# Another order of ScalarE's and VectorE's work in the columns with table building

## The chip, the cores and the metric

The kernel runs on one core of a Trainium2 chip, in one launch. A core has five engines that run side by side and meet at semaphores: TensorE (matmul), VectorE, ScalarE, GpSimd and SyncE, each taking its own instructions strictly in order. The metric is the device time of one execution in microseconds, the median of some runs. Beside it stands one execution that the hardware profiler recorded.

## The reference, cut to what matters

A two-layer block (four gated feed-forward parts, a pooling and a convolution mixer) is followed by a block with attention, a recurrent part and, at the end, a layer of 16384 single-neuron experts. The change lies in this last layer, `peer_ffn`:

```python
s = jnp.einsum('thpk,hpnk->thpn', q, sub_keys)
top_s, top_i = lax.top_k(s, PEER_TOPK)
...
best_s, best_pos = lax.top_k(cand_s, PEER_TOPK)
idx = jnp.take_along_axis(cand_i, best_pos, axis=-1)
g = jax.nn.softmax(best_s, axis=-1)
u = jnp.take(expert_u, idx, axis=0)
v = jnp.take(expert_v, idx, axis=0)
act = jax.nn.gelu(jnp.einsum('td,thkd->thk', xc, u))
return jnp.einsum('thk,thkd->td', (g * act).astype(v.dtype), v)
```

There are 512 tokens in four tiles of 128; each token picks 8 x 16 = 128 of the 16384 experts, all in fp32 with 1024 features.

## The kernel before

For the last 384 tokens the kernel computes the layer densely. All experts lie in 128 columns of 128. In the *up* stage each column is a weight group of 512 KB that gives the activations of 128 experts for 384 tokens. In the *down* stage these are multiplied by a table of each token's expert weights, and by the second weights. The first 128 tokens are done sparsely: GpSimd gathers, for each of the 128 picks, the 128 rows that the tokens chose (`gather`, L492, 512 KB each, through a `ring` of 4 slots), and VectorE takes the dot product with the tokens (`dot`, L1371). A slot comes free with its dot, and then the next gather goes out.

A weight group passes through these steps. SyncE loads it to `raw` (four slots, L449; a load waits until the group four before it has its low part). ScalarE rounds it to `whi` (`hi`, L511), VectorE takes the rest `wlo` (`low`, L1359), both three columns (LOOK) ahead of TensorE. TensorE makes three matmuls for each of eight blocks (L1520 to L1522, 24 in a column). ScalarE applies the activation function to the result (`column`, L804: act_out) and has it stored to HBM (`store_acts`, L796).

The table for the dense tokens is built in the up stage too, in 3 batches (one for each token tile) of 16 chunks of 8 tokens. A chunk rides on one up column. VectorE writes two one-hot tensors (`rows`, L1458 hot_m and L1459 hot_n). ScalarE scales hot_m by the weights, eight instructions (`weigh`, L825: hot_w). TensorE multiplies hot_n by hot_w, 8 matmuls, 16 passes in the trace (`sums`, L1811), and ScalarE writes the sums to the table `spread` in two halves (`take_rows`, L833). hot_m, hot_n, hot_w and the banks of the sums are double. The semaphore hot_used counts finished sums: the one-hot tensors of chunk c+2 wait for the sums of c.

The order of work is written out by hand for each engine. After a batch of 16 chunks stands a gap of 8, 8 and 16 plain columns (GAPS), in which the 8 MB of `spread` are spilled to HBM (L853; in the last gap L856 and L857). The next batch's first `weigh` waits for the spill. The 128 dots are spread over chunks and gaps; after the last of them the first tokens' activations can be computed. TensorE runs a column and then that chunk's sums.

Of the kernel before, what the change touches and what calls it, by code (L numbers as in the profile page):

```python
# [107 lines left out]
CHUNKS = P // TC  # L108
# [14 lines left out]
def at(c, i, m):  # L123

    return c if i is None else i * m + c
# [7 lines left out]
def build(nc, stream, ada, c_rows, smalls, consts, smalls2, consts2, keys, u_rows, xin, out):  # L133
# [289 lines left out]
    def hot_column(of, c):  # L423
        return of[:, TC * c:TC * c + TC].unsqueeze(2).to_broadcast([P, TC, P])
# [10 lines left out]
    with nc.Block() as block:  # L435
# [66 lines left out]
        def _(act):  # L502
            def hi(c, i=None, m=0):

                if c >= n_groups:
                    return
                s = c % R
                act.wait_ge(raw_landed[s], at(16 * (c // R + 1), i, 16 * m // R))
                if c >= R:
                    act.wait_ge(pe_groups, at(c - R + 1, i, m))  # L510
                act.activation(whi[:, s, :, :], raw[:, s, :, :], ACT.Copy).then_inc(hi_ready, 1)  # L511
# [286 lines left out]
            def column(m, i, first=True):  # L798
                if first:
                    hi(up + m + LOOK, i, 4)  # L800
                act.wait_ge(pe_groups, at(up + m + 1, i, 4))
                if m >= 4:
                    act.wait_ge(acts_stored[m % 4], at(16 * (m // 4), i, 16))
                act.activation(act_out[:, m % 4, :], psum[4 + m % 4][:, 0:TD], ACT.Gelu_apprx_tanh).then_inc(gelu_done, 1)  # L804
                if m:
                    store_acts(m - 1, i)

            def columns_run(m0, n):

                if m0 == 0:  # L810
                    for m in range(4):
                        column(m, None)
                    m0, n = 4, n - 4
                with act.Fori(0, n // 4) as i:
                    for m in range(m0, m0 + 4):
                        column(m, i)

            def weigh(c):

                s = c % 2  # L820
                act.wait_ge(hot_mark, c + 1)
                if c >= 2:
                    act.wait_ge(hot_used, c - 1)
                for k in range(TC):
                    ins = act.activation(hot_w[:, s, k, :], hot_m[:, s, k, :], ACT.Copy, scale=pick_w[:, TC * c + k:TC * c + k + 1])  # L825
                ins.then_inc(weights_ready, 1)

            def take_rows(c):

                act.wait_ge(hot_used, c + 1)  # L830
                for half in range(2):
                    k = TC * (c % CHUNKS) + 4 * half
                    act.activation(spread[:, :, k:k + 4].rearrange("p m t -> p t m"),  # L833
                                   psum[2 * (c % 2) + half][:, :].rearrange("p (t m) -> p t m", t=4), ACT.Copy).then_inc(spread_ready, 1)
# [5 lines left out]
            for j in range(DT):  # L840
                if j:
                    act.wait_ge(spilled, 16 * j)
                weigh(CHUNKS * j)
                for k in range(CHUNKS):
                    c = CHUNKS * j + k
                    hi(up + CHUNK_AT[j] + k + LOOK)
                    if k + 1 < CHUNKS:
                        weigh(c + 1)
                    column(CHUNK_AT[j] + k, None, False)
                    take_rows(c)  # L850
                act.wait_ge(spread_ready, 2 * CHUNKS * (j + 1))
                if j < DT - 1:
                    act.dma_start(expert_weights[j], spread[:, :, :]).then_inc(spilled, 16)  # L853
                    columns_run(CHUNK_AT[j] + CHUNKS, GAPS[j])
                else:
                    act.dma_start(expert_weights[j][:, 0:EARLY, :], spread[:, 0:EARLY, :]).then_inc(spilled, 16)  # L856
                    act.dma_start(expert_weights[j][:, EARLY:NK, :], spread[:, EARLY:NK, :]).then_inc(spilled_late, 16)  # L857
# [60 lines left out]
        def _(dve):  # L918
# [444 lines left out]
            def low(n=1):  # L1363
                for c in range(cursor[0], cursor[0] + n):
                    lo(c)
                cursor[0] += n

            def dot(n=1):
                for q in range(cursor[1], cursor[1] + n):
                    dve.wait_ge(ring_landed[q % RING], 16 * (q // RING + 1))  # L1370
                    dve.tensor_tensor_reduce(ring[:, q % RING, :], ring[:, q % RING, :], h_row[:, :], 1.0, 0.0, ALU.mult, ALU.add,  # L1371
                                             dots[:, q:q + 1]).then_inc(ring_used, 1)
                cursor[1] += n
# [79 lines left out]
            def rows(c):  # L1453
                s = c % 2
                if c >= 2:
                    dve.wait_ge(hot_used, c - 1)
                numbers = iota_b[:, :].unsqueeze(1).to_broadcast([P, TC, P])
                dve.tensor_tensor(hot_m[:, s, :, :], numbers, hot_column(pick[:, 1, :], c), ALU.is_equal).then_inc(hot_mark, 1)  # L1458
                dve.tensor_tensor(hot_n[:, s, :, :], numbers, hot_column(pick[:, 0, :], c), ALU.is_equal).then_inc(hot_ready, 1)  # L1459

            for j in range(DT):
                for k in range(CHUNKS):
                    rows(CHUNKS * j + k)
                    low()
                    dot(2)
                for k in range(GAPS[j] - 4 * (j == DT - 1)):
                    low()
                    dot()

            down = SEG["down"][0]  # L1470

            def out_step(m):

                dve.wait_ge(g_landed[m % 4], 16 * (m // 4 + 1))
                dve.wait_ge(a_landed[m % 4], 16 * (m // 4 + 1))
                if m >= 2:
                    dve.wait_ge(we_ready, m - 1)
                dve.tensor_tensor(we32[:, m % 2, :], act_in[:, m % 4, :], g_ring[:, m % 4, :], ALU.mult).then_inc(we_mul, 1)
                if m >= AHEAD:
                    low()  # L1480
                dve.wait_ge(we_hi_ready, m + 1)
                dve.tensor_tensor(we[:, m % WSLOTS, 1, :], we32[:, m % 2, :], we[:, m % WSLOTS, 0, :].bitcast(F32),
                                  ALU.subtract).then_inc(we_ready, 1)
# [9 lines left out]

            for k in range(4):
                low()
                dot()
                if k:
                    out_step(k - 1)
            assert cursor == [down + AHEAD, PICKS]
# [459 lines left out]
```

## Time and profile before

| | |
|---|---|
| median of 3 runs | 3652.83 us (3651.1 to 3654.18) |
| profiled execution | 3660.15 us, span 3658.2 us |
| TensorE busy | 3286.6 us (90%) |
| VectorE busy | 1987.1 us (54%) |
| ScalarE busy | 1323.1 us (36%) |
| GpSimd busy | 1357.7 us (37%) |
| granted TensorE clock, mean | 0.940 of 2.4 GHz |
| HBM traffic | 636.86 MB, mean 174 GB/s |
| up stage with its table building | about 2475 to 3125 us |

The span runs from the first to the last instruction; the profiled execution's own time is 2 us more. Busy shares are means over stages with different limits, so a stage is to be read by itself: who waits there, and for whom.

### The profile page before, as it was taken

What the parts mean: (1) busy time and instruction counts of PE and PEld (TensorE: products, weight loads), DVE (VectorE), ACT (ScalarE), POOL (GpSimd) and SP (SyncE); (2) the same over time, 40 slices, a digit from 0 to 9 for tenths busy, and PEclk for the clock granted to TensorE, in tenths of its full rate; (3) what the DMA queues carried; (4) which work ended last, traced back from release to release, by engine and by line L of the source; (5) the groups of instructions that cost most, each with busy time, mean ns of one, the idle gap of its engine ahead of it and who ended that gap; (6) DMA issues with size and microseconds to landing.
All of it is one profiled execution on the core that took longest, in us unless ns stands there. A gap on an engine that the chain in (4) does not pass through costs nothing.

```text
span 3658.2 us, 44563 instructions
## 1 busy us (share of the span) xinstructions
PE 3286.6 (90%) x15088; PEld 2804.3 (77%) x15088; DVE 1987.1 (54%) x2967; ACT 1323.1 (36%) x1959; POOL 1357.7 (37%) x654
## 2 busy tenths in 40 slices
PE   4999689998999899999788789997877778999999
PEld 3888568886888687888566578997777778888887
DVE  6552465405550435110476768775555554688887
ACT  3322233213322323222345432445545454333333
POOL 3444244443444443444222034563333332132221
PEclk9999889999999999999898699998888889999999
DMA  5554145423552222222121032455675858899997
GB/s 224 194 193 150 58 138 195 166 98 127 195 180 96 81 98 88 98 98 98 52 69 47 14 108 98 160 164 180 219 255 174 299 174 334 317 360 364 362 363 280
DMA packets 234647, 636.86 MB, mean 174 GB/s; under 512 B 22560, under 2 KB 104736, under 8 KB 233504
## 3 DMA queue, kind: packets, MB, share of 16 engines
q1 hardware_dynamic: 87408, 318.49, 25.4%
q10 hardware_dynamic: 110256, 182.59, 14.1%
q0 software_dynamic: 36864, 134.23, 11.0%
q8 instruction: 71, 1.16, 0.1%
q14 instruction: 48, 0.39, 0.0%
HBM read 580.69 MB, written 54.53 MB: 174 GB/s over the span
## 4 chain that ended last, share of the span: by engine, by line
issue 37%; PE 28%; POOL 16%; DVE 8%; ACT 7%; DMA 3%; ACTq 0%; POOLq 0%; DVEq 0%
POOL wlo L473 16%; PE bank L1850 5%; PE bank L1851 5%; PE bank L1852 5%; PE bank L1520 3%; PE bank L1522 3%; PE bank L1521 3%; DVE ring L1371 3%; ACT hot_w L825 2%; ACT spread L833 2%; DMA ring<-u_rows_dram,cell_u 2%; DVE wlo L1359 2%; DVE hot_m L1458 2%; ACT whi L511 1%; PE bank L1717 1%
## 5 line engine op out<-in xcount | busy, mean ns | idle before, releaser
L473 POOL TENSOR_TENSOR wlo<-raw,whi 128x1024 fp32r<-128x1024 f32 x394 | 1001.9, 2544 | 1467.2 <-ACT whi L511 1466.8
L1520 PE MATMUL bank<-hhi,whi 128*128 128x512 f32 (+1 forms) x2832 | 1068.3, 377 | 53.2 <-DVE wlo L1359 21.5
L1521 PE MATMUL bank<-hlo,whi 128*128 128x512 f32 (+1 forms) x2832 | 1056.0, 373 | 0.0
L1522 PE MATMUL bank<-hhi,wlo 128*128 128x512 f32 (+1 forms) x2832 | 1054.7, 372 | 0.0
L511 ACT ACTIVATE whi<-raw 128x1024 fp32r<-128x1024 f32 x599 | 633.2, 1058 | 1010.7 <-PE bank L1522 618.7
L1520 PEld LDWEIGHTS bank<-hhi,whi 128*128 128x128 f32 x2832 | 542.2, 191 | 128.9 <-DVE wlo L1359 22.5
L1521 PEld LDWEIGHTS bank<-hlo,whi 128*128 128x128 f32 x2832 | 540.8, 191 | 71.8 <-issue 1.4
L1522 PEld LDWEIGHTS bank<-hhi,wlo 128*128 128x128 f32 x2832 | 539.0, 190 | 71.8
L1359 DVE TENSOR_TENSOR wlo<-raw,whi 128x1024 fp32r<-128x1024 f32 x205 | 251.3, 1226 | 319.9 <-ACT whi L511 300.5
L925 DVE CUSTOM_DVE_ANT_0 ada_raw<-ada_raw,cond_row 128x1024 f32<-128x1024 f32 x128 | 301.3, 2385 | 155.9 <-DMA ada_raw<-ada_dram 155.7
L492 POOL DMA_INDIRECT ring<-u_rows_dram,cell_u x128 | 215.7, 1685 | 417.2 <-DVE dots L1371 400.8
L1850 PE MATMUL bank<-whi,we 128*128 128x512 f32 x768 | 299.7, 390 | 5.1 <-issue 5.1
L1851 PE MATMUL bank<-whi,we 128*128 128x512 f32 x768 | 299.5, 390 | 0.0
L1852 PE MATMUL bank<-wlo,we 128*128 128x512 f32 x768 | 299.4, 390 | 0.0
L492 POOL DMA_INDIRECT ring<-stream_dram,cell_v x128 | 139.9, 1093 | 384.8 <-DVE y L1490 358.7
L1520 PE MATMUL bank<-uhi,whi 128*128 (+1 forms) x704 | 273.9, 389 | 0.0
L1521 PE MATMUL bank<-ulo,whi 128*128 (+1 forms) x704 | 273.9, 389 | 0.0
L1522 PE MATMUL bank<-uhi,wlo 128*128 (+1 forms) x704 | 273.9, 389 | 0.0
L1811 PE MATMUL bank<-hot_w,hot_n 128*128 128x128 f32 x768 | 154.0, 383 | 118.4 <-issue 117.5
L1811 PEld LDWEIGHTS bank<-hot_w,hot_n 128*128 128x128 f32 x768 | 144.2, 289 | 132.0 <-issue 132.0
L991 DVE TENSOR_TENSOR u<-silu,bank 128x512 f32<-128x512 f32 x88 | 60.5, 687 | 302.1 <-PE bank L1522 239.2
L563 ACT ACTIVATE uhi<-u 128x512 f32 (+1 forms) x88 | 55.6, 632 | 407.1 <-DVE u L991 407.1
(244 smaller groups left out, 3817.6 us busy)
## 6 DMA issues: line engine op xcount, KB each, us to landing
raw<-stream_dram SPq DMA_DIRECT2D x599, 512.0 KB
ada_raw<-ada_dram ACTq DMA_DIRECT2D x128, 512.0 KB, 4.1
expert_acts<-act_out ACTq DMA_DIRECT2D x128, 192.0 KB
g_ring<-expert_weights ACTq DMA_DIRECT2D x128, 192.0 KB
act_in<-expert_acts ACTq DMA_DIRECT2D x128, 192.0 KB
first_raw<-ada_dram ACTq DMA_DIRECT2D x8, 1024.0 KB, 23.4
expert_weights<-spread ACTq DMA_DIRECT2D x2, 4096.0 KB, 21.0
x<-xin_dram SPq DMA_DIRECT2D x1, 2048.0 KB, 12.5
```

The costliest lines, as they stand in the source:

```text
L473: pool.tensor_tensor(wlo[:, s, :, :], raw[:, s, :, :], whi[:, s, :, :].bitcast(F32), ALU.subtract).then_inc(lo_ready, 1)
L492: pool.indirect_dma_start(ring[:, q % RING, :], None, rows, bass.IndirectOffsetOnAxis(ap=cell[:, c:c + 1], axis=0)).then_inc(ring_landed[q ...
L511: act.activation(whi[:, s, :, :], raw[:, s, :, :], ACT.Copy).then_inc(hi_ready, 1)
L925: dve.tensor_tensor_reduce(ada_raw[:, u % 2, :], ada_raw[:, u % 2, :], cond_row[:, :], 1.0, 0.0, ALU.mult, ALU.add, ada_dot[:, u % KT:u % ...
L1359: dve.tensor_tensor(wlo[:, s, :, :], raw[:, s, :, :], whi[:, s, :, :].bitcast(F32), ALU.subtract).then_inc(lo_ready, 1)
L1520: pe.matmul(bank, whi[:, s, b, :], rhi, start=start, stop=False)
L1521: pe.matmul(bank, whi[:, s, b, :], rlo, start=False, stop=False)
L1522: return pe.matmul(bank, wlo[:, s, b, :], rhi, start=False, stop=stop)
L1811: mm = pe.matmul(out, hot_n[:, s, k, :], hot_w[:, s, k, :], start=True, stop=True)
L1850: pe.matmul(bank, we[:, m % WSLOTS, 0, toks], rh, start=m == 0, stop=False, skip_group_check=True)
L1851: pe.matmul(bank, we[:, m % WSLOTS, 1, toks], rh, start=False, stop=False, skip_group_check=True)
L1852: mm = pe.matmul(bank, we[:, m % WSLOTS, 0, toks], rl, start=False, stop=last, skip_group_check=True)
```

## The change

ScalarE: in a batch the two instructions that write chunk c-1 to `spread` stand behind the next column's whi, ahead of hot_w; before, those of chunk c stood behind act_out of the same column. VectorE: the one-hot tensors of chunk c+1 are made ahead of the low part of chunk c's column; before, those of chunk c, and the batch begins with those of its first chunk. In place of two dots a chunk column has one and two by turns, and a gap column has two, every fourth one, in place of one. No instruction is added or removed; 24 of the 128 dots move from the chunk columns to the gaps.

```diff
@@ ScalarE @@
                     hi(up + CHUNK_AT[j] + k + LOOK)
+                    if k:
+                        take_rows(c - 1)
                     if k + 1 < CHUNKS:
                         weigh(c + 1)
                     column(CHUNK_AT[j] + k, None, False)
-                    take_rows(c)
+                take_rows(CHUNKS * j + CHUNKS - 1)
                 act.wait_ge(spread_ready, 2 * CHUNKS * (j + 1))
@@ VectorE @@
             for j in range(DT):
+                rows(CHUNKS * j)
                 for k in range(CHUNKS):
-                    rows(CHUNKS * j + k)
+                    if k + 1 < CHUNKS:
+                        rows(CHUNKS * j + k + 1)
                     low()
-                    dot(2)
+                    dot(1 + k % 2)
                 for k in range(GAPS[j] - 4 * (j == DT - 1)):
                     low()
-                    dot()
+                    dot(2 - (k % 4 == 3))
...
             for k in range(4):
                 low()
-                dot()
+                dot(2 - (k == 3))
                 if k:
                     out_step(k - 1)
```

ScalarE in the third chunk of the first batch, before (in the names, the number is that of the tensor; bank2 and bank3 hold one chunk's sums, bank0 and bank1 the other's; what an instruction waits for stands in brackets):

```order
L511 ACTIVATE whi_50<-raw_49 128x1024 [waits pe_groups,raw_landed0]
L825 ACTIVATE hot_w_141<-hot_m_140,pick_w_143 128x128 [waits hot_used,hot_mark]
L825 ACTIVATE hot_w_141<-hot_m_140,pick_w_143 128x128 x7
L804 ACTIVATE act_out_155<-bank6 128x384 [waits acts_stored2,pe_groups]
L796 DMA expert_acts<-act_out_155 128x384 [waits gelu_done]
L833 ACTIVATE spread_153<-bank0 128x4x128 [waits hot_used]
L833 ACTIVATE spread_153<-bank1 128x4x128
L511 ACTIVATE whi_50<-raw_49 128x1024 [waits pe_groups,raw_landed1]
```

And after, from the same whi on:

```order
L511 ACTIVATE whi_50<-raw_49 128x1024 [waits pe_groups,raw_landed0]
L833 ACTIVATE spread_153<-bank2 128x4x128 [waits hot_used]
L833 ACTIVATE spread_153<-bank3 128x4x128
L825 ACTIVATE hot_w_141<-hot_m_140,pick_w_143 128x128 [waits hot_used,hot_mark]
L825 ACTIVATE hot_w_141<-hot_m_140,pick_w_143 128x128 x7
L804 ACTIVATE act_out_155<-bank6 128x384 [waits acts_stored2,pe_groups]
L796 DMA expert_acts<-act_out_155 128x384 [waits gelu_done]
L511 ACTIVATE whi_50<-raw_49 128x1024 [waits pe_groups,raw_landed1]
```

The two rows that write `spread` now stand ahead of hot_w and empty the banks of the chunk before (bank2 and bank3) in this column; those of bank0 and bank1 follow in the next.

VectorE in the third chunk of the same batch, from its one-hot tensors to the next (a dot is two rows, the product and the read of its sum), before:

```order
L1458 TENSOR_TENSOR hot_m_140<-iota_b_138,pick_142 128x1024 [waits hot_used]
L1459 TENSOR_TENSOR hot_n_139<-iota_b_138,pick_142 128x1024
L1359 TENSOR_TENSOR wlo_51<-raw_49,whi_50 128x1024 [waits hi_ready]
L1371 ISA ring_152,dots_150<-ring_152,h_row_149 128x1024 [waits ring_landed0]
L1371 ISA dots_150 128x1
L1371 ISA ring_152,dots_150<-ring_152,h_row_149 128x1024 [waits ring_landed1]
L1371 ISA dots_150 128x1
L1458 TENSOR_TENSOR hot_m_140<-iota_b_138,pick_142 128x1024 [waits hot_used]
L1459 TENSOR_TENSOR hot_n_139<-iota_b_138,pick_142 128x1024
```

And after, over two chunks, the first with one dot:

```order
L1460 TENSOR_TENSOR hot_m_140<-iota_b_138,pick_142 128x1024 [waits hot_used]
L1461 TENSOR_TENSOR hot_n_139<-iota_b_138,pick_142 128x1024
L1361 TENSOR_TENSOR wlo_51<-raw_49,whi_50 128x1024 [waits hi_ready]
L1373 ISA ring_152,dots_150<-ring_152,h_row_149 128x1024 [waits ring_landed3]
L1373 ISA dots_150 128x1
L1460 TENSOR_TENSOR hot_m_140<-iota_b_138,pick_142 128x1024 [waits hot_used]
L1461 TENSOR_TENSOR hot_n_139<-iota_b_138,pick_142 128x1024
L1361 TENSOR_TENSOR wlo_51<-raw_49,whi_50 128x1024 [waits hi_ready]
L1373 ISA ring_152,dots_150<-ring_152,h_row_149 128x1024 [waits ring_landed0]
L1373 ISA dots_150 128x1
```

Before, two dots stand between a low part and the next one-hot tensors; now one or two. The rows read alike, but the one-hot tensors ahead of a column's low part are now those of the next chunk, not of that column's.

VectorE in the first columns of the first gap, before:

```order
L1359 TENSOR_TENSOR wlo_51<-raw_49,whi_50 128x1024 [waits hi_ready]
L1371 ISA ring_152,dots_150<-ring_152,h_row_149 128x1024 [waits ring_landed0]
L1371 ISA dots_150 128x1
L1359 TENSOR_TENSOR wlo_51<-raw_49,whi_50 128x1024 [waits hi_ready]
L1371 ISA ring_152,dots_150<-ring_152,h_row_149 128x1024 [waits ring_landed1]
L1371 ISA dots_150 128x1
```

And after:

```order
L1361 TENSOR_TENSOR wlo_51<-raw_49,whi_50 128x1024 [waits hi_ready]
L1373 ISA ring_152,dots_150<-ring_152,h_row_149 128x1024 [waits ring_landed2]
L1373 ISA dots_150 128x1
L1373 ISA ring_152,dots_150<-ring_152,h_row_149 128x1024 [waits ring_landed3]
L1373 ISA dots_150 128x1
L1361 TENSOR_TENSOR wlo_51<-raw_49,whi_50 128x1024 [waits hi_ready]
L1373 ISA ring_152,dots_150<-ring_152,h_row_149 128x1024 [waits ring_landed0]
L1373 ISA dots_150 128x1
L1373 ISA ring_152,dots_150<-ring_152,h_row_149 128x1024 [waits ring_landed1]
L1373 ISA dots_150 128x1
```

A gap column's low part is now followed by two dots, each with its own slot of the ring, and the next low part stands behind both.

## Rows read from the trace of the kernel before

In the rows PE is TensorE, DVE VectorE, ACT ScalarE, POOL GpSimd. A wait put down to "issue" is one for which the profile shows no releaser.

**Rows 1.** Waits, 2475 to 3125 us: who waited for whom, total us, times, longest.
```profile
DVE wlo L1359 <- ACT whi L511: 231.6, 71, 6.6
...
ACT hot_w L825 <- DVE hot_m L1458: 221.7, 48, 4.7
...
PE bank L1811 <- issue: 117.5, 46, 5.5
...
DVE ring L1371 <- DMA ring<-u_rows_dram,cell_u: 56.5, 11, 19.1
```

**Rows 2.** Stretches: from:to, length, busy us (instructions) per engine, PEclk, DMA share, GB/s.
```profile
2489.00:2631.00 142.00, 106.03 (x547) 101.94 (x545) 81.04 (x98) 75.92 (x167) 51.14 (x28) 0.84 0.58 171
...
2635.00:2679.00 44.00, 37.91 (x208) 37.59 (x208) 21.54 (x28) 14.20 (x18) 12.58 (x9) 0.92 0.97 386
...
3040.00:3125.00 85.00, 72.44 (x396) 71.45 (x396) 43.40 (x58) 28.45 (x38) 22.75 (x17) 0.92 0.99 387
```

**Rows 3.** Timeline of one chunk: start us, us, engine, line, operation [idle before <-releaser].
```profile
2552.84 1.23 DVE L1359 TENSOR_TENSOR wlo<-raw,whi 128x1024 fp32r<-128x1024 f32 x1 [4.38 <-ACT whi L511]
...
2553.98 1.22 DVE L1371 CUSTOM_DVE_ANT_0 ring<-ring,h_row 128x1024 f32<-128x1024 f32 x1
...
2555.12 1.22 DVE L1371 CUSTOM_DVE_ANT_0 ring<-ring,h_row 128x1024 f32<-128x1024 f32 x1
...
2556.27 1.22 DVE L1458 TENSOR_TENSOR hot_m<-iota_b,pick 128x1024 bf16<-128x1024 bf16 x1
...
2557.52 0.40 ACT L825 ACTIVATE hot_w<-hot_m,pick_w 128x128 f32<-128x128 bf16 x1 [4.72 <-DVE hot_m L1458]
...
2559.87 0.47 ACT L804 ACTIVATE act_out<-bank 128x384 f32<-128x384 f32 x1
...
2560.07 3.60 PE L1811 MATMUL bank<-hot_w,hot_n 128*128 128x128 f32 x16 [2.36 <-issue]
...
2560.24 1.91 ACT L833 ACTIVATE spread<-bank 128x512 f32<-128x512 f32 x2
...
2561.95 1.05 ACT L511 ACTIVATE whi<-raw 128x1024 fp32r<-128x1024 f32 x1
...
2563.03 1.22 DVE L1359 TENSOR_TENSOR wlo<-raw,whi 128x1024 fp32r<-128x1024 f32 x1 [4.41 <-ACT whi L511]
```

**Rows 4.** Timeline, TensorE, the first chunks of the first batch.
```profile
2480.30 1.95 PE L1811 MATMUL bank<-hot_w,hot_n 128*128 128x128 f32 x16
...
2482.00 0.42 PE L1520 MATMUL bank<-hhi,whi 128*128 128x384 f32 x1
...
2487.26 2.02 PE L1811 MATMUL bank<-hot_w,hot_n 128*128 128x128 f32 x16 [0.85 <-ACT hot_w L825]
```

**Rows 5.** Stretches, the table sums of the chunk in rows 3.
```profile
2560.00:2563.30 3.30, 3.23 (x16) 3.26 (x17) 0.27 (x1) 3.00 (x4) 0.00 (x0) 0.54 0.77 239
```

**Rows 6.** Timeline, TensorE: last, first, last, first and last table sums.
```profile
2631.39 3.27 PE L1811 MATMUL bank<-hot_w,hot_n 128*128 128x128 f32 x16 [2.35 <-issue]
...
2683.51 3.47 PE L1811 MATMUL bank<-hot_w,hot_n 128*128 128x128 f32 x16 [3.10 <-issue]
...
2834.69 2.02 PE L1811 MATMUL bank<-hot_w,hot_n 128*128 128x128 f32 x16 [1.47 <-issue]
...
2887.12 3.03 PE L1811 MATMUL bank<-hot_w,hot_n 128*128 128x128 f32 x16 [2.59 <-issue]
...
3037.91 3.57 PE L1811 MATMUL bank<-hot_w,hot_n 128*128 128x128 f32 x16 [2.37 <-issue]
```

**Rows 7.** Timeline, VectorE and GpSimd, the first gap.
```profile
2663.66 1.23 DVE L1371 CUSTOM_DVE_ANT_0 ring<-ring,h_row 128x1024 f32<-128x1024 f32 x1 [17.21 <-DMA ring<-u_rows_dram,cell_u]
...
2668.17 0.94 POOL L492 DMA_INDIRECT ring<-u_rows_dram,cell_u  x1 [1.32 <-DVE dots L1371]
...
2678.51 1.23 DVE L1371 CUSTOM_DVE_ANT_0 ring<-ring,h_row 128x1024 f32<-128x1024 f32 x1 [0.34 <-DMA ring<-u_rows_dram,cell_u]
```

**Rows 8.** Groups of instructions, 2475 to 3125 us: count, busy us, mean ns, idle before.
```profile
L492 POOL DMA_INDIRECT ring<-u_rows_dram,cell_u x124 | 211.8, 1708 | 416.1 <-DVE dots L1371 400.8 <-issue 15.3
```

## The prediction, made before the changed kernel ran

> **What bounds the kernel now.** I read the waits of the table-building stretch first [rows 1]. VectorE waits 231.6 us for ScalarE's whi, ScalarE 221.7 us for VectorE's hot_m, and TensorE stands before its table sums (L1811) 46 times, for 117.5 us. Two engines that wait for each other by turns, with a third that waits for both, is a ring of work and not a full engine. The busy times by stage say the same [rows 2]: from 2489 to 2631 us TensorE is busy 106.03 of 142 us, VectorE 81.04 and ScalarE 75.92, at 171 GB/s. In the gap columns after it (2635 to 2679) the DMA share is 0.97 at 386 GB/s, and in the last gap (3040 to 3125) 0.99 at 387 GB/s. So there are two kinds of stretch: chunk columns bound by the ring, gap columns bound by transfers.
>
> The timeline of one chunk shows the ring closed [rows 3]. VectorE splits a weight group (wlo, 2552.84), takes two dots (2553.98 and 2555.12), makes hot_m (2556.27). Then ScalarE starts hot_w (2557.52), act_out (2559.87), spread (2560.24) and whi (2561.95), and only that releases the next wlo at 2563.03. One turn is 2563.03 - 2552.84 = 10.19 us: VectorE's four pitches of about 1.14 and ScalarE's 2.35 + 0.37 + 1.71 + 1.08, one after the other. The program does not require that: a low part is three columns ahead of TensorE, and a spread half has a bank of its own until two chunks later. It is the order on the two in-order engines alone that ties them.
>
> TensorE's need is in rows too. Early in the first batch the table sums run from 2480.30, the next column from 2482.00, and the next sums from 2487.26 after 0.85 us of idle [rows 4]: sums 1.70, column 2487.26 - 0.85 - 2482.00 = 4.41, together 6.11 us. Later the sums start after 2.36 us of idle [rows 3], and the stretch from 2560.0 to 2563.3 has a granted clock of 0.54 (about 1.2 GHz) for them, 3.3 us long [rows 5]. The idle therefore costs twice.
>
> **The change, part by part.** *ScalarE.* spread of chunk c-1 now stands behind whi of the next column and ahead of hot_w, in place of spread of c behind act_out. Nothing is added: per chunk 2.35 + 0.37 + 1.71 + 1.08 = 5.5 us of issue-to-issue time [rows 3]. The store of the activations keeps its place behind act_out. What spread waits for (the sums of c-1) and what hot_w waits for is now the same event, the end of these sums. Queued behind that wait are hot_w(c+1), needed by TensorE a full period later, and the next act_out and whi, needed three columns later. So a late spread delays nobody until it is late by about a period. The price of this move is 0 as long as ScalarE's turn fits into TensorE's. Let T be the end of a sum: spread and hot_w end near T + 4.2, act_out waits for the column that ends at T + 4.4 and ends near T + 5.0, whi near T + 6.2, and then the next sums are just over. It fits, barely; in place of the column it would free-run at 5.5.
>
> *VectorE.* hot_m/hot_n of chunk c+1 go ahead of the low part instead of behind the dots, one chunk earlier in the row, and a chunk has 1 or 2 dots, 1.5 in the mean, in place of 2. Need per chunk: hot 2 x 1.14, low 1.14, dots 1.5 x 1.145, together 5.1 us, 5.7 in a chunk with two dots [rows 3]. It also waits for the sums' end, has hot_m at T + 1.3, before ScalarE's spread is through (T + 1.8), and its low part finds a whi that is already written. Once per batch two hot pairs stand ahead of the first low, 2.3 us later, against three columns of lead: 0.
>
> With ring and cover gone the period is the largest of TensorE's 6.0 to 6.1 and the 5.5 and 5.1 of the others, plus what the semaphores cost. I take 6.1; the bounds are 6.0 and, if ScalarE's turn of 6.2 picks up a hand-over at each end, 6.6. Before, sums start 2480.30 and 2631.39 in batch one [rows 4, 6]: 151.09 / 15 = 10.07. Batch two 2683.51 to 2834.69 is 10.08, batch three 2887.12 to 3037.91 is 10.05 [rows 6]. There are 45 such intervals: 45 x (10.07 - 6.1) = 178.7 us. The last sums of batches one and three shrink from 3.27 and 3.57 to about 1.95 [rows 4, 6]: 2.9 more. Together **-181 us**.
>
> The clock enters that sum. By the row, sums after 2.36 us of idle run at a clock of 0.54 [rows 3, 5], and sums without or with 0.85 of idle take 1.95 to 2.02 [rows 4]. Were they at 1.2 GHz without idle too, the period would be 4.41 + 3.3 = 7.7 and the sum 45 x (10.07 - 7.7) = 107. The Trainium skill, TensorE: Matmul & The Clock Gate, part 1, says that "the default state is throttled, and activity releases the throttle"; by that rule the denser chunks hold 2.4 GHz and the 6.1 stands, and these rows agree.
>
> *The gaps.* 24 dots move from the chunks to the gap columns: 14, 14 and 28 stand there in place of 8, 8 and 16, each with a gather of 128 rows x 4 KB = 0.524 MB behind it through a ring of four. This is the price, since the gaps are where transfers bind. In the first gap before, two dots go at once, and then VectorE stands 17.21 us for a gather behind the table's spill; the dots start at 2663.66 and the sixth after it is the last at 2678.51 [rows 7]: (2678.51 - 2663.66) / 5 = 2.97 us per dot and column. A gather issued by GpSimd at 2668.17 is used at 2678.51, 10.3 us later [rows 7]. After the change VectorE does its last chunk's dots early, since it no longer waits there, so all four slots should be full at the spill: 4 dots go at once and 10 stand behind it instead of 6. If bytes set the pace (a weight group 0.524 MB, a column's activations 128 x 384 x 4 = 0.197), a column is 0.524 + 0.197 + 1.75 x 0.524 = 1.64 MB against 1.245, 2.97 x 1.64 / 1.245 = 3.91 us for 1.75 dots, or 2.24 per dot: the tail is 9 x 2.24 = 20.1 in place of 14.9, +5.3. If each gather keeps its 2.97, it is 26.7, +11.9. I take +8, twice: +16, bounds 10 and 24. What is late next is hot_m of the next batch, then its first sums. In the last gap 12 dots are added, less two full slots: 10 x 0.524 MB / 387 GB/s [rows 2] = 13.5 us. TensorE works through part of that stretch, so 0 to 5 is the lower end; 10 x 2.97 = 30 is the upper. I take +13.5. Together **+29.5 us**.
>
> The raw loads on SyncE's queue wait for low parts that come as early or earlier, and GpSimd, at 1.71 us an issue [rows 8], has 4 us per gather in the chunks. In the chunks the transfers rise to (0.524 + 0.197 + 1.5 x 0.524) MB / 6.1 us = 247 GB/s, under the 386 that the gap shows: 0.
>
> Sum: -181 + 29.5 = -151.5 us. The profiled execution took 3660.15 us (span 3658.2), so 3508.7; the median of the runs shown is 7.3 us lower, 3652.83, and 3652.83 - 151.5 is **3501 us**, 4.1% faster. The down stage is unchanged and starts when the last columns are done.
>
> **The rivals.**
>
> 1. *Gathers cost more (0.18).* For it: 10.3 us from issue to use, a full DMA share, and VectorE's in-order queue, where a low part now stands behind two dots. Against it: with four gathers in flight dots came every 2.97. If a gather comes only every 4.1 us, as three queues sharing 386 GB/s evenly would give it (0.524 / 0.129), the two tails cost (9 x 4.1 - 14.9) x 2 = 44 more and the last gap's ten 10 x 4.1 = 41: +85, so -96, 3557 us. The Trainium skill, DMA: Bandwidth & Descriptors, "Queues, rings and completion order", has each transfer engine go round-robin between its queues by packet, which would make such an even share. The trace does not quite agree: VectorE stands 17.21 us for a gather [rows 7] whose transfer should by then have had its share beside the spill's.
>
> 2. *Another ring in the chunks (0.13).* spread and hot_w now both wait for the sums; if the hand-overs add up, or the sums stay at 1.2 GHz, the period is 7.7: -107 + 29.5 = -77, 3575 us. For it: ScalarE's 6.2 against TensorE's 6.1. Against: every hand-over has a spare buffer, so only loads, not latencies, should count.
>
> 3. *Slower (0.04).* The place is the gaps. If every one of the 24 moved dots exposed a whole gather, 10.3 us, with low parts and TensorE behind it, that is 247 us against 181: +66, 3719 us. It decides from 181 / 24 = 7.5 us per moved dot. The pace of 2.97 speaks against it. TensorE's own lead of three columns hides the first of them.
>
> 4. *The change does nothing (0.02).* Were hot_used late for VectorE (sums behind whi behind low), the turn would stay at 10. The order of the rows speaks against it: no whi or low part is behind the same chunk's hot_m any more.
>
> My forecast holds 0.63.
>
> **How the numbers follow.** The forecast's own range: period 6.0 and gaps +12 give -174 (3479); period 6.6 and gaps +54 give 45 x 3.47 + 3 - 54 = -105 (3548). The range 3475 to 3565 takes in rival 1 and leaves out 2 to 4, 0.19. A difference of 0.2% (7 us) is about what a measurement of this kernel tells from none. Faster by more: the forecast and rivals 1 and 2, 0.94; within it 0.02; slower 0.04.
>
> **What would show it.** In the profile after: sums every 6.0 to 6.6 us, 1.7 to 2 us long, at a granted clock near 1.0; ScalarE's wait for hot_m and VectorE's for whi near zero in the chunks; TensorE without idle before L1811. The three batches end 55 to 60 us earlier each. The gaps grow from 49 us between the last and next first sums [rows 6] to 54 to 61, with VectorE's waits for the ring above the 56.5 us of now [rows 1] and still the DMA share of 0.97. I am wrong if the sums still take 3.3 us, if a period over 7 appears, or if a gap passes 70 us.

## The result, and the profile after

The changed kernel takes 3493.47 us (median of 4 runs, 3489.53 to 3497.5) against 3652.88 us before (4 runs). The ratio is 0.9564, 95% interval 0.9547 to 0.9581: 159.4 us or 4.4% less, where 151.5 us less was forecast. Its profiled execution took 3489.53 us, span 3487.6.

The waits of the stretch with table building, 2475 to 2970 us, who waited for whom:

```profile
DVE ring L1373 <- DMA ring<-u_rows_dram,cell_u: 78.2, 27, 18.5
...
ACT act_out L804 <- DMA expert_acts<-act_out: 55.0, 8, 18.0
...
DVE wlo L1361 <- ACT whi L511: 31.8, 11, 7.3
...
ACT hot_w L825 <- DVE hot_m L1460: 16.0, 2, 8.6
...
PE bank L1524 <- DVE wlo L1361: 28.8, 3, 10.7
...
PE bank L1854 <- ACT act_out L804: 14.6, 1, 14.6
...
PE bank L1815 <- issue: 13.8, 2, 7.5
```

The waits of before in [rows 1] are those of the same part of the program, which took longer then. VectorE's wait for whi has gone from 231.6 to 31.8 us, ScalarE's for hot_m from 221.7 to 16.0, TensorE's before the sums from 117.5 in 46 waits to 13.8 in two [rows 1]. VectorE's wait for gathers has grown from 56.5 to 78.2, and act_out still stands 55.0 us for stores (65.6 before). The ring is gone and the transfers stay. What TensorE waits for now lies in the gaps and at their end: 28.8 us for low parts (21.5 before) and 14.6 us ahead of the first matmul of the down stage, L1854 (5.1 before).

The stretches of the first batch, the first gap, and the last gap (PE, PEld, DVE, ACT, POOL busy, then granted clock, DMA share, GB/s):

```profile
2474.00:2565.00 91.00, 91.00 (x613) 91.00 (x612) 76.04 (x89) 84.34 (x176) 31.18 (x23) 1.00 0.84 277
...
2565.00:2616.00 51.00, 33.37 (x183) 32.73 (x182) 27.09 (x38) 12.07 (x21) 20.42 (x14) 0.86 0.96 370
...
2861.00:2955.00 94.00, 71.71 (x391) 70.52 (x390) 54.51 (x77) 27.50 (x37) 38.39 (x28) 0.88 1.02 405
```

In the batch TensorE is busy 91.00 of 91.00 us at a clock of 1.00; before, it was 106.03 of 142 at 0.84 [rows 2]. ScalarE, at 84.34 of 91, is close behind. The transfers rose from 171 to 277 GB/s there and are at their limit only in the gaps, as before.

One chunk in order of time:

```profile
2521.62 1.95 PE L1815 MATMUL bank<-hot_w,hot_n 128*128 128x128 f32 x16
...
2523.61 2.01 ACT L833 ACTIVATE spread<-bank 128x512 f32<-128x512 f32 x2 [0.28 <-PE bank L1815]
...
2523.61 1.23 DVE L1460 TENSOR_TENSOR hot_m<-iota_b,pick 128x1024 bf16<-128x1024 bf16 x1 [0.16 <-PE bank L1815]
...
2525.41 2.42 ACT L825 ACTIVATE hot_w<-hot_m,pick_w 128x128 f32<-128x128 bf16 x8
...
2525.89 1.22 DVE L1361 TENSOR_TENSOR wlo<-raw,whi 128x1024 fp32r<-128x1024 f32 x1
...
2527.02 1.22 DVE L1373 CUSTOM_DVE_ANT_0 ring<-ring,h_row 128x1024 f32<-128x1024 f32 x1
...
2527.57 1.95 PE L1815 MATMUL bank<-hot_w,hot_n 128*128 128x128 f32 x16
...
2527.77 0.49 ACT L804 ACTIVATE act_out<-bank 128x384 f32<-128x384 f32 x1
...
2528.22 1.06 ACT L511 ACTIVATE whi<-raw 128x1024 fp32r<-128x1024 f32 x1
...
2529.55 1.22 DVE L1460 TENSOR_TENSOR hot_m<-iota_b,pick 128x1024 bf16<-128x1024 bf16 x1 [1.31 <-PE bank L1815]
```

The sums repeat after 5.95 us (2521.62, 2527.57) and last 1.95. Their end lets spread and hot_m go in the same moment, 2523.61. hot_m is done at 2524.84, 0.57 us before hot_w (2525.41) wants it, and the low part at 2525.89 waits for nothing. These are the steps of [rows 3] with no chain through both engines left. In this chunk, with one dot, VectorE even waits 1.31 us for the next sums.

The first and last sums of each batch, TensorE:

```profile
2468.10 1.95 PE L1815 MATMUL bank<-hot_w,hot_n 128*128 128x128 f32 x16
...
2557.30 1.95 PE L1815 MATMUL bank<-hot_w,hot_n 128*128 128x128 f32 x16
...
2616.56 3.75 PE L1815 MATMUL bank<-hot_w,hot_n 128*128 128x128 f32 x16 [7.48 <-issue]
...
2708.36 1.95 PE L1815 MATMUL bank<-hot_w,hot_n 128*128 128x128 f32 x16
...
2767.46 3.75 PE L1815 MATMUL bank<-hot_w,hot_n 128*128 128x128 f32 x16 [6.37 <-issue]
...
2858.93 1.95 PE L1815 MATMUL bank<-hot_w,hot_n 128*128 128x128 f32 x16
```

Fifteen intervals are 89.20 us in batch one against 151.09 before, 91.80 and 91.47 in the others against 151.18 and 150.79 [rows 4, 6]. The later two are longer by one slow start: their first sums come after 7.48 and 6.37 us of idle and take 3.75 us.

VectorE in the first gap, dots only:

```profile
2564.14 1.22 DVE L1373 CUSTOM_DVE_ANT_0 ring<-ring,h_row 128x1024 f32<-128x1024 f32 x1
...
2568.72 1.22 DVE L1373 CUSTOM_DVE_ANT_0 ring<-ring,h_row 128x1024 f32<-128x1024 f32 x1
...
2589.54 1.23 DVE L1373 CUSTOM_DVE_ANT_0 ring<-ring,h_row 128x1024 f32<-128x1024 f32 x1 [18.46 <-DMA ring<-u_rows_dram,cell_u]
...
2611.58 1.21 DVE L1373 CUSTOM_DVE_ANT_0 ring<-ring,h_row 128x1024 f32<-128x1024 f32 x1
```

Four dots go by 2568.72 at their own pace. The fifth waits 18.46 us behind the spill, and the last ten start between there and 2611.58: (2611.58 - 2589.54) / 9 = 2.45 us each.

### The profile page after: what moved, and what is told of

It is laid out like the page before. It is cut to its first block, busy times and chain, and to the rows that moved or that the text cites. A ratio compares the mean times of both kernels' runs of the same rounds, so it can differ in the third digit from the quotient of the medians.

```text
span 3487.6 us, 44563 instructions
## 1 busy us (share of the span) xinstructions
PE 3200.6 (92%) x15088; PEld 2733.2 (78%) x15088; DVE 1991.2 (57%) x2967; ACT 1329.8 (38%) x1959; POOL 1312.2 (38%) x654
## 3 DMA queue, kind: packets, MB, share of 16 engines
q0 software_dynamic: 36864, 134.23, 10.7%
## 4 chain that ended last, share of the span: by engine, by line
issue 39%; PE 36%; POOL 17%; DMA 4%; DVE 3%; ACT 1%; POOLq 0%; ACTq 0%; DVEq 0%
POOL wlo L473 17%; PE bank L1854 5%; PE bank L1856 5%; PE bank L1855 5%; PE bank L1524 5%; PE bank L1525 5%; PE bank L1526 5%; DMA ring<-u_rows_dram,cell_u 4%; PE bank L1815 3%; DVE ring L1373 1%; PE bank L1721 1%; POOL ring L492 0%; DVE wlo L1361 0%; DVE rstd L966 0%; DVE sp L1279 0%
## 5 line engine op out<-in xcount | busy, mean ns | idle before, releaser
L1524 PE MATMUL bank<-hhi,whi 128*128 128x512 f32 (+1 forms) x2832 | 1062.4, 375 | 60.2 <-DVE wlo L1361 28.8
L1854 PE MATMUL bank<-whi,we 128*128 128x512 f32 x768 | 299.8, 390 | 14.6 <-ACT act_out L804 14.6
L1856 PE MATMUL bank<-wlo,we 128*128 128x512 f32 x768 | 299.5, 390 | 0.0
L492 POOL DMA_INDIRECT ring<-u_rows_dram,cell_u x128 | 171.7, 1341 | 310.6 <-DVE dots L1373 295.4
L1373 DVE CUSTOM_DVE_ANT_0 ring<-ring,h_row 128x1024 f32<-128x1024 f32 x128 | 153.7, 1220 | 80.7 <-DMA ring<-u_rows_dram,cell_u 78.2
L1854 PEld LDWEIGHTS bank<-whi,we 128*128 128x128 f32 x768 | 144.7, 188 | 44.8 <-issue 14.8
```

What stands on the lines that cost most here:

```text
L492: pool.indirect_dma_start(ring[:, q % RING, :], None, rows, bass.IndirectOffsetOnAxis(ap=cell[:, c:c + 1], axis=0)).then_inc(ring_landed[q ...
L1524: pe.matmul(bank, whi[:, s, b, :], rhi, start=start, stop=False)
L1854: pe.matmul(bank, we[:, m % WSLOTS, 0, toks], rh, start=m == 0, stop=False, skip_group_check=True)
L1856: mm = pe.matmul(bank, we[:, m % WSLOTS, 0, toks], rl, start=False, stop=last, skip_group_check=True)
```

## The experiments

Medians are of the runs of each kernel; the ratio is always to the kernel before. One thing has to be known to compare traces: the stretch ahead of the first batch is the same code in all kernels, yet its last softmax step (expo) starts at 2460.3 us in one profiled execution and 2471.5 in another. So beside the medians I compare the time from that step to the end, the *region*: 1186.7 us before, 1027.3 after, -159.4.

### ScalarE's part alone

```diff
                     hi(up + CHUNK_AT[j] + k + LOOK)
+                    if k:
+                        take_rows(c - 1)
...
                     column(CHUNK_AT[j] + k, None, False)
-                    take_rows(c)
+                take_rows(CHUNKS * j + CHUNKS - 1)
```

> Only ScalarE's part of the change: spread of the chunk before stands ahead of hot_w; VectorE's order and its dots as before. Theory A (the turn of 10.07 us is a sum over two in-order engines, and spread's 1.71 us leaves it once it stands where ScalarE waits for VectorE anyway): one turn is VectorE's low, two dots and hot_m (4.6 to 4.7) plus hot_w, act_out and whi (2.35 + 0.37 + 1.05), 8.4 to 8.5 us; 45 x (10.07 - 8.45) = 73, gaps unchanged: 3580 us (3570 to 3595). Theory B (only VectorE's order ties the ring, ScalarE's place for spread does nothing): turn 10.1, 3650 us. Theory C (ScalarE's order is what opens the ring): turn 6, 3475 us.

Measured: 3583.35 us, ratio 0.9813 (0.9791 to 0.9835). The sums come every 8.48 us. ScalarE and VectorE in one chunk:

```profile
2519.88 0.47 ACT L804 ACTIVATE act_out<-bank 128x384 f32<-128x384 f32 x1
...
2520.25 1.04 ACT L511 ACTIVATE whi<-raw 128x1024 fp32r<-128x1024 f32 x1
...
2521.19 2.05 ACT L833 ACTIVATE spread<-bank 128x512 f32<-128x512 f32 x2
...
2521.32 1.23 DVE L1361 TENSOR_TENSOR wlo<-raw,whi 128x1024 fp32r<-128x1024 f32 x1 [2.70 <-ACT whi L511]
...
2526.01 0.40 ACT L825 ACTIVATE hot_w<-hot_m,pick_w 128x128 f32<-128x128 bf16 x1 [2.77 <-DVE hot_m L1460]
```

The ring is still closed: whi (2520.25) releases the low part (2521.32), two dots and hot_m follow, and hot_w starts 2.77 us late at 2526.01. But spread (2521.19) now lies beside VectorE's work. A turn has lost just that: turns of 10.2 us in the steady part of a batch are 8.5 now. Theory A, 8.4 to 8.5 us and 3580, holds.

### VectorE's new place for the one-hot tensors alone

```diff
             for j in range(DT):
+                rows(CHUNKS * j)
                 for k in range(CHUNKS):
-                    rows(CHUNKS * j + k)
+                    if k + 1 < CHUNKS:
+                        rows(CHUNKS * j + k + 1)
                     low()
                     dot(2)
```

> Only VectorE's new place for the one-hot tensors (a chunk earlier, ahead of the low part); ScalarE's order as before, dots as before (two in a chunk, one in a gap column). Theory A (with the one-hot tensors ready early, hot_w no longer waits, and what is left is ScalarE's own 5.5 us after the end of the sums, under TensorE's 5.95): sums every 5.95 us at full clock; 45 x (10.07 - 5.95) = 185, less 5 for slow first chunks, gaps as before: 3473 us (3465 to 3490), so that ScalarE's part of the change is not needed. Theory B (both halves are needed, since spread behind act_out waits for the sums of its own column and holds up whi and the low part): turn of 7.5 or more, 3540 us or above.

Measured: 3464.90 us, ratio 0.9486 (0.9466 to 0.9507). Fifteen intervals take 89.2 to 89.3 us in all three batches, 5.95 each. This one edit does more than the whole change: it opens the ring by itself, and it leaves the dots in the chunks. Theory A holds, just under the lower end of its range.

### The change without ScalarE's part

The edit above with the change's dots (one or two in a chunk, mostly two in a gap column).

> The changed kernel without ScalarE's part: VectorE's new order and the moved dots, ScalarE's order as before. Theory A (ScalarE's part does nothing once VectorE's is there): as the changed kernel, 3493 us (3485 to 3500). Theory B (ScalarE's part buys slack that the busier gaps need): 3505 us or more.

Measured: 3500.61 us, ratio 0.9581 (0.9563 to 0.9599), 7 us above the changed kernel, with intervals that overlap. The chunks are the same 5.95 us. The region is 1039.0 us against 1027.3, in gaps of 61.2 and 61.5 us against 59.3 and 59.1 and an end 6 us longer. So in the chunks ScalarE's part is worth nothing. The median lies between the two theories, so whether it is worth some microseconds in the busier gaps stays open.

### Both orders, dots as they were

> Both engines' new order, but the dots stay where they were before (two in a chunk, one in a gap column). Theory A (the moved dots cost 7 us in each of the first two gaps and 8 in the last, and VectorE's 5.7 us with two dots still fits into TensorE's 5.95): the chunks keep their 5.95 us, the gaps are back at 52 us, 22 us less than the changed kernel: 3471 us (3463 to 3480). Theory B (two gathers in 5.95 us, 297 GB/s in all, or VectorE at 5.7, do not fit, so the move of the dots pays for itself): the period goes to 6.4 or more, 3490 us or above.

Measured: 3460.15 us, ratio 0.9474 (0.9456 to 0.9492), 33.3 us under the changed kernel. The chunks keep 5.95 us with two dots, and VectorE does not wait for a gather anywhere in the stage. The gaps (first sums after less last sums before) are 49.2 and 49.6 us instead of 59.3 and 59.1, and from the last sums to the end it is 618.5 instead of 628.7: 10.1 + 9.5 + 10.2 = 29.8, and 3.1 more in the batches, mostly slow first sums; the region says 31.8 in all. That is the price of the moved dots, 33.3 / 24 = 1.4 us each in the mean; in the traces it is 10.1 and 9.5 us for six dots in each of the first two gaps, 1.6 to 1.7 each, and 10.2 for twelve in the last, 0.9 each. Theory A was right on the period and put the price too low, at 22 us, so the median lies under its range.

This run and the one with VectorE's part alone differ only by ScalarE's part. It brings 4.8 us in the medians (3464.90 to 3460.15), where the runs of the second kernel alone scatter over 9 us, and 0.5 us in the region (996.0 to 995.5). With the dots in the chunks no gain of ScalarE's part is shown.

What bounds the gap that is left, waits in the first gap:

```profile
DVE wlo L1361 <- ACT whi L511: 27.2, 6, 16.4
...
ACT act_out L804 <- DMA expert_acts<-act_out: 19.0, 3, 16.8
...
PE bank L1524 <- DVE wlo L1361: 5.2, 1, 5.2
```

act_out stands up to 16.8 us for a store behind the spill, whi and the low part stand behind act_out, and TensorE behind these, 5.2 us instead of 10.7 in the changed kernel.

### The dots alone

```diff
-                    dot(2)
+                    dot(1 + k % 2)
...
-                    dot()
+                    dot(2 - (k % 4 == 3))
...
-                dot()
+                dot(2 - (k == 3))
```

> Only the dots move (one or two in a chunk, mostly two in a gap column); both orders as before. Theory A (a dot is part of the ring, and a moved gather costs 0.9 us in the gaps): a turn loses half a dot, 0.57 us, 45 x 0.57 = 26 less, and the gaps cost 22 more: 3649 us (3640 to 3656). Theory B (the gaps are bound by the spill alone and the moved gathers hide in them): 3627 us. Theory C (a moved gather exposes its 10 us): 3700 us or more.

Measured: 3669.53 us, ratio 1.0040 (1.0024 to 1.0056), slower, above theory A's 3656. Sums at the end of the first batch and the start of the second:

```profile
2598.04 2.02 PE L1811 MATMUL bank<-hot_w,hot_n 128*128 128x128 f32 x16 [1.26 <-issue]
...
2608.27 3.76 PE L1811 MATMUL bank<-hot_w,hot_n 128*128 128x128 f32 x16 [4.02 <-issue]
...
2617.33 2.02 PE L1811 MATMUL bank<-hot_w,hot_n 128*128 128x128 f32 x16 [0.36 <-issue]
...
2682.78 3.75 PE L1811 MATMUL bank<-hot_w,hot_n 128*128 128x128 f32 x16 [7.17 <-issue]
```

Turns of 9.07 and 10.2 us by turns, a dot of 1.14 less in every second, as said: 7.7 to 9.2 us less in a batch. The gap from 2617.33 to 2682.78 is where it failed: 65.5 us, and 63.7 in the second, against 52.1 and 52.4, so +13.3 and +11.2, where theory A has 0.9 us for each of six dots. The same dots moved under the new orders cost 10.1 and 9.5 (the run above). VectorE's first wait of the gap:

```profile
2650.99 1.23 DVE L1371 CUSTOM_DVE_ANT_0 ring<-ring,h_row 128x1024 f32<-128x1024 f32 x1 [22.00 <-DMA ring<-u_rows_dram,cell_u]
```

With VectorE's old order the last two dots of the batch start at 2621.46 and 2622.61, when the spill is issued (2622.64), so their gathers stand behind it. After two dots of the gap the ring is empty, and 12 dots come after a wait of 22.00 us, 2.44 us apart, where the changed kernel has 10 after 18.46. As far as these two comparisons show, a moved dot costs more where the ring is not full at the spill.

### Twice as many dots moved

```diff
-                    dot(1 + k % 2)
+                    dot()
...
-                    dot(2 - (k % 4 == 3))
+                    dot(3 - k % 2)
...
-                dot(2 - (k == 3))
+                dot(3 - k % 2)
```

> The changed kernel with 24 dots more moved from the chunks to the gaps (one in a chunk column, three and two by turns in a gap column): the suspected price doubled. Theory A (a gather moved to a gap costs its bytes, 0.524 MB / 390 GB/s = 1.34 us, since the transfers bind there): 24 x 1.34 = 32 more, 3526 us (3515 to 3535), the sums still every 5.95 us. Theory B (it costs a landing of its own, 2.45 us): 3552 us. Theory C (it hides): 3495 us.

Measured: 3530.18 us, ratio 0.9663 (0.9648 to 0.9677), 36.7 us above the changed kernel, 1.5 us for each of the 24, just over theory A's 32 and far from B and C. The gaps are 68.4 and 69.2 us, 9.1 and 10.1 more for six dots each. The sums still come every 5.95 us. So a gather moved into a gap costs a little more than the 1.34 us that its 0.524 MB take at the 390 GB/s that all transfers share there; what the rest is stays open.

### The spill in eight pieces

```diff
                 if j < DT - 1:
-                    act.dma_start(expert_weights[j], spread[:, :, :]).then_inc(spilled, 16)
-                    columns_run(CHUNK_AT[j] + CHUNKS, GAPS[j])
+                    for g in range(GAPS[j]):
+                        act.dma_start(expert_weights[j][:, 16 * g:16 * g + 16, :], spread[:, 16 * g:16 * g + 16, :]).then_inc(spilled, 16)
+                        column(CHUNK_AT[j] + CHUNKS + g, None)
```

The waits for the spill count eight pieces for each of these two gaps.

> Both orders, old dots, and in the first two gaps the 8.4 MB spill goes out in eight pieces, one ahead of each gap column's act_out, in place of one transfer. Theory A (in the gaps TensorE stands because act_out waits for stores queued behind the whole spill): stores and gathers now land between the pieces, act_out's wait of 17 us is gone and a gap shrinks from 49.4 us (first sums after it less last sums before) towards 18.3 MB / 390 GB/s = 47 or, where transfers run over into the chunks, 42 to 46: 3450 us (3442 to 3458). Theory B (the bytes alone bind the gap): 48 to 50 us a gap, 3460 us.

Measured: 3472.81 us, ratio 0.9518 (0.9501 to 0.9535), 12.7 us slower than the spill in one. Waits in the first gap:

```profile
PE bank L1816 <- issue: 14.9, 1, 14.9
...
ACT act_out L804 <- DMA expert_acts<-act_out: 12.0, 3, 6.0
...
ACT hot_w L825 <- DMA expert_weights<-spread: 10.3, 1, 10.3
```

act_out's longest wait has fallen from 16.8 to 6.0 us as theory A said, but both theories missed what comes next: the last piece goes out a column before the batch, and hot_w, which waits for the whole spill, stands 10.3 us for it, TensorE 14.9. The gaps are 54.3 and 55.4 us, in place of 49.2 and 49.6.

### The later wait for the spill, without and with the pieces

```diff
-                if j:
-                    act.wait_ge(spilled, 16 * j)
                 weigh(CHUNKS * j)
...
+                    if j and k == 1:
+                        act.wait_ge(spilled, 16 * j)
                     if k:
                         take_rows(c - 1)
```

> Both orders, old dots, the spill as one transfer, and only the later wait for the spill. Theory A (the later wait matters only where the spill is stretched over the gap): as both orders with the old dots, 3460 us, gaps of 49 to 50 us. Theory B (the wait is what the first hot_w stands for there too): 3455 us, gaps of 45 us.

Measured, the later wait with the spill in one: 3461.43 us, ratio 0.9476 (0.9463 to 0.9489), gaps of 49.5 and 49.4 us. No difference, theory A.

> As the split spill, and ScalarE waits for the spill only ahead of the next batch's first write to spread, not ahead of its first hot_w. Theory A: the end of the spill is then hidden behind one chunk more, another 0 to 4 us a gap: 3446 us (3438 to 3458). Theory B (the bytes bind): no difference to the split spill.

Measured, with the pieces (the count is 16 * 8 * j): 3454.93 us, ratio 0.9463 (0.9448 to 0.9478). The first gap's waits and its stretch:

```profile
ACT act_out L804 <- DMA expert_acts<-act_out: 10.4, 2, 5.4
...
PE bank L1816 <- issue: 5.0, 1, 5.0
```

```profile
2560.00:2604.00 44.00, 39.29 (x233) 38.97 (x231) 23.50 (x28) 17.20 (x27) 9.27 (x10) 0.98 1.02 405
```

TensorE's wait before the first sums is 5.0 us in place of 14.9, and the gaps are 44.4 and 45.3 us. The transfers are at 405 GB/s. Against the spill in one (3460.15) it is 5 us less, with intervals that overlap. Against the run that differs by the pieces alone (3461.43) it is 6.5 us less, the region is 988.5 us against 995.8, and the gaps 44.4 and 45.3 against 49.5 and 49.4: the gain is real, though only with both edits. Theory B is out, since the split spill alone took 3472.81.

### The last gap's spill in pieces too

> As the split spill with the late wait (3455 us), and the last gap's spill in eight pieces too. Theory A (in the last gap, too, act_out stands 18.6 us for a store behind the spill and TensorE 7 us behind that): the end after the last sums shrinks from 618.2 us by 3 to 7: 3450 us (3443 to 3456). Theory B (the bytes bind the last gap): no change, 3455 us.

Measured: 3453.58 us, ratio 0.9451 (0.9438 to 0.9464). From the last sums to the end it is 615.0 us instead of 618.2. The last gap's waits:

```profile
ACT act_out L804 <- DMA expert_acts<-act_out: 24.2, 6, 5.7
...
PE bank L1856 <- ACT act_out L804: 9.4, 1, 9.4
```

act_out's longest wait is 5.7 instead of 18.6 us, but the first matmul of the down stage (L1856) then stands 9.4 us behind the last act_out, where it stood 4.7 us with the last spill in one. The expected 3 to 7 are 3.2 in the trace and 1.4 in the medians, within the noise of these, so the medians do not decide between the theories. This is the lowest median of the study, 40 us under the changed kernel, and not told apart from the 3454.93 before it.

## Why the prediction was right, point by point

**The ring and its end.** The reading of [rows 3] as a sum over two in-order engines was right to the term. ScalarE's part alone takes spread's 1.7 us out of the turn (from the 10.19 of [rows 3] to 8.48), and VectorE's part alone opens it (5.95). Forecast were 6.1 us, bounds 6.0 to 6.6; 5.95 was measured, just under the lower bound. With the sums' 1.70 the column is 4.25 us and not the 4.41 that I took from [rows 4], which counted its last matmul to the end.

**The chunks, -181 us.** The intervals between sums gave 61.9 + 59.4 + 59.3 = 180.6 us where 178.7 was said. Two misses cancel, and that is luck: 45 x 0.15 = 7 us more from the shorter period, and some 5 us less since the first sums of batches two and three come cold after an idle gap, which the sum had left out.

**The clock.** The table sums take 1.95 us at a granted clock of 1.00 once nothing is idle ahead of them, where those of [rows 3] took 3.60, with a granted clock of 0.54 in their stretch [rows 5]. The 7.7 us period of rival 2 does not occur. But "the idle therefore costs twice" did not hold in the kernel before. In its second batch slow and fast sums took turns:

```profile
2712.06 2.02 PE L1811 MATMUL bank<-hot_w,hot_n 128*128 128x128 f32 x16 [1.58 <-issue]
...
2722.29 3.75 PE L1811 MATMUL bank<-hot_w,hot_n 128*128 128x128 f32 x16 [4.04 <-issue]
...
2732.51 2.02 PE L1811 MATMUL bank<-hot_w,hot_n 128*128 128x128 f32 x16 [1.57 <-issue]
```

Both kinds come 10.2 us after the one before. While the ring set the pace, a slow sum only took up time in which TensorE would have stood. The sum did not use that sentence, so the forecast did not suffer.

**ScalarE's turn fits.** In the chunk shown spread waits 0.28 us for the sums' end and whi ends 5.67 us later (2523.61 to 2529.28), where the text had said 6.2, in a period of 5.95. The price of 0 holds; but the text let the move pass as half of the remedy. With VectorE's part there it gains nothing in the chunks.

**The gaps, +29.5 us.** Four slots full at the spill, ten dots behind it, 2.45 us each between the bounds 2.24 and 2.97: as said. From last to first sums the gaps grew by 7.1 and 6.7 us (said: 8 less up to 1.3 for the shorter sums), and the end by 8.4 (said: 13.5 less 1.6). Without the shorter last sums this growth over the kernel before is 8.5 + 6.7 + 10.0 = 25.2 us. Measured against the same orders with the old dots, the moved dots cost 33 us; the new order alone had made the first two gaps 3 us shorter each, which the sum did not have. That 29.5 lies between the two is luck in part. The end was the one term clearly over-sized, by 3.5 us.

**The sum.** Of the 7.9 us between -151.5 and -159.4, 3.5 are that end, about 2 the chunks, and about 2 the gaps and the entry.

**The rivals.** Dearer gathers (1) would have needed a gather every 4.1 us and gaps of some 73 us from sums to sums; they come every 2.45 us and the gaps are 59. The even share between queues did not show: one gather waits 18.46 us beside a spill on another queue. The slower case (3) was off by the factor it had to overcome: a moved dot costs 1.4 us where 7.5 decides. Without effect (4) the turn would have stayed at 10; it is 5.95.

## What to carry to other kernels

When two in-order engines wait for each other by turns, add up the turn from one timeline and look for the instruction whose input is ready a step earlier; moving that one may open the ring alone, and the rest of a rewrite should be tried without. Work that moves out of a stretch lands in another: here the ring was opened with two dots still in it, and taking half a dot out of each chunk, into columns bound by transfers, gave back 33 of 193 us. A slow instruction inside a wait that something else sets costs nothing: before counting what it costs, look whether fast and slow ones come at the same interval. In this kernel a bulk transfer cut in pieces helped the small ones behind it, and the time only when whoever waits for its end waited later too.

## What the runs showed of the hardware

The same idle does not always lower the clock. With ScalarE's part alone, two sums after 2.27 us of idle:

```profile
2503.09 2.02 PE L1813 MATMUL bank<-hot_w,hot_n 128*128 128x128 f32 x16 [2.27 <-issue]
...
2537.03 3.56 PE L1813 MATMUL bank<-hot_w,hot_n 128*128 128x128 f32 x16 [2.27 <-issue]
```

One takes 2.02 us at a granted clock of 1.00 and one 3.56 at 0.54, in the same loop; after 0.64 to 0.87 us of idle every one takes 2.02. Before the change, those of [rows 6] after 2.35 us or more of idle took 3.03 to 3.57, and the one after 1.47 took 2.02.

A transfer of 8.4 MB holds up small ones that are issued behind it, by the same engine and by another. In the changed kernel's first gap ScalarE issues the spill at 2561.31 and GpSimd a gather at 2565.64. The dot that needs this gather starts at 2589.54, after 18.46 us of waiting. The store that act_out waits for, issued by ScalarE like the spill, holds it for 18.0 us. Before the change the first gap's spill took 26.4 us from issue to landing. With both orders and the old dots, act_out's longest wait in the first gap falls from 16.8 to 6.0 us when the spill goes out in eight pieces.
